# A four-block transformer kernel: memory layer and compressed attention spread beside other TensorE work, last feed-forward chunks token tile outer

## What is computed

```python
# first block, each layer
hf = swiglu(rms_norm(x, g[0]), w_gate[layer, 0], w_up[layer, 0], w_down[layer, 0])
x = x + 0.5 * rms_norm(hf, g[1]);  xn = rms_norm(x, g[2])
x = x + rms_norm(mixer(xn), g[3])
...                                   # second FFN with g[4], g[5]
# memory layer
qk, v, o, gates = split(xn @ w_in)
q, k = split(silu(causal_depthwise_conv(qk, conv_w)))      # 4 taps
hid = h_num / maximum(abs(n_num), exp(-m_t))               # per head
hid = hid * rsqrt(mean(hid * hid) + EPS) * head_g * sigmoid(o)
# second block, layer 0: compressed attention
blocks = t[:, :, win_idx, :] + pos        # 15 blocks of 32 tokens, stride 16
cmp = gelu(flat(blocks) @ w1) @ w2        # once for keys, once for values
o_c = masked_softmax(q @ k_cmp * scale + bias) @ v_cmp
o = sigmoid(g0) * o_c + sigmoid(g1) * o_selected + sigmoid(g2) * o_window
```

## Time and profile before

| | us |
|---|---|
| median of 3 runs | 2490.64 (2482.09 to 2491.22) |
| the profiled execution, its own time | 2498.82 |
| its span from first to last instruction | 2497.0 |
| PE busy | 2196.6 (88%) |
| DVE busy | 1714.2 (69%) |
| ACT busy | 1077.2 (43%) |
| GpSimd (POOL) busy | 711.0 (28%) |

### The profile page before, as it was taken

The page is one execution under the profiler, slowest core; times in us unless marked ns, Lnnn a source line. Parts: engine busy times, 40 slices in busy tenths (PEclk is TensorE's granted clock), DMA queues, the critical chain, the costliest instruction groups (busy, mean ns, idle before and its releaser), DMA issues.

```text
span 2497.0 us, 30819 instructions
## 1 busy us (share of the span) xinstructions
PE 2196.6 (88%) x13056; PEld 1916.5 (77%) x13056; DVE 1714.2 (69%) x1351; ACT 1077.2 (43%) x1097; POOL 711.0 (28%) x350
## 2 busy tenths in 40 slices
PE   7997978998998955899897869999998877999996
PEld 6896958998998944899795758777777556777775
DVE  5897346997998456699723666777774346767766
ACT  4433455334334423433432435655552334645544
POOL 2898004995996000499400000000000000000000
PEclk9998988999999976999897879999998778999998
DMA  9776505876786620678551036787774104877773
GB/s 330 264 261 212 183 23 200 277 258 215 264 270 205 186 86 9 217 264 279 190 158 62 1 118 225 281 286 278 264 245 150 34 18 153 305 260 275 270 255 115
DMA packets 281913, 495.95 MB, mean 199 GB/s; under 512 B 11816, under 2 KB 167576, under 8 KB 281616
## 3 DMA queue, kind: packets, MB, share of 16 engines
q1 hardware_dynamic: 257952, 410.19, 48.9%
q0 software_dynamic: 23552, 82.75, 9.2%
q10 hardware_dynamic: 272, 1.05, 0.1%
HBM read 486.56 MB, written 12.10 MB: 200 GB/s over the span
## 4 chain that ended last, share of the span: by engine, by line
PE 75%; DVE 13%; DMA 5%; ACT 4%; issue 3%; ACTq 0%; DVEq 0%; SPq 0%
PE psum L901 72%; DMA ring<-in_moe_w_up 3%; DVE nrm L1845 3%; DVE low L1845 2%; ACT wh L1505 2%; DMA ring<-in_ffn_w_up 2%; PE psum L961 1%; DVE hl L1845 1%; DVE wide L2225 1%; DVE xl L1845 1%; PE psum L1113 1%; DVE wide L1845 1%; DMA ring<-in_moe_w_down 1%; DMA ring<-in_moe_w_gate 0%; DVE aux L1845 0%
## 5 line engine op out<-in xcount | busy, mean ns | idle before, releaser
L1845 DVE TENSOR_TENSOR low<-ring,wh 128x2048 fp32r<-128x2048 f32 x386 | 1072.5, 2800 | 402.3 <-ACT wh L1505 402.2
L1505 ACT ACTIVATE wh<-ring 128x2048 fp32r<-128x2048 f32 x386 | 733.4, 1906 | 720.0 <-PE psum L901 323.1
L901 PE MATMUL psum<-xh,wh 128*128 128x256 f32 x1832 | 522.3, 285 | 6.7 <-DVE xl L1845 4.3
L901 PE MATMUL psum<-xh,low 128*128 128x256 f32 x1832 | 522.9, 285 | 0.0
L901 PE MATMUL psum<-xl,wh 128*128 128x256 f32 x1832 | 520.7, 284 | 0.0
L712 POOL TENSOR_TENSOR big<-big 128x1024 f32<-128x1024 f32 x144 | 374.7, 2602 | 11.3
L901 PEld LDWEIGHTS psum<-xh,wh 128*128 128x128 f32 x1832 | 353.0, 193 | 12.8 <-issue 8.3
L901 PEld LDWEIGHTS psum<-xl,wh 128*128 128x128 f32 x1832 | 352.0, 192 | 1.5
L901 PEld LDWEIGHTS psum<-xh,low 128*128 128x128 f32 x1832 | 352.2, 192 | 0.0
L901 PE MATMUL psum<-wh,xh 128*128 128x256 f32 (+5 forms) x864 | 279.2, 323 | 11.9 <-DVEq L617 5.8
L901 PE MATMUL psum<-wh,bigr 128*128 128x512 f32 x768 | 255.9, 408 | 23.3 <-DVE hl L1845 23.3
(11 more groups left out here) (326 smaller groups left out, 2536.0 us busy)
## 6 DMA issues: line engine op xcount, KB each, us to landing
ring<-in_moe_w_gate SPq DMA_DIRECT2D x64, 1024.0 KB, 5.3
ring<-in_moe_w_up SPq DMA_DIRECT2D x64, 1024.0 KB, 5.9
ring<-in_moe_w_down SPq DMA_DIRECT2D x64, 1024.0 KB, 5.1
big<-in_ada_w POOLq DMA_DIRECT2D x48, 1024.0 KB, 6.6
ring<-in_ffn_w_gate SPq DMA_DIRECT2D x44, 1024.0 KB, 5.4
ring<-in_ffn_w_up SPq DMA_DIRECT2D x44, 1024.0 KB, 5.5
ring<-in_ffn_w_down SPq DMA_DIRECT2D x44, 1024.0 KB, 5.7
ring<-in_mlstm_w_in SPq DMA_DIRECT2D x16, 1024.0 KB, 5.6
```

The costliest lines, as they stand in the source:

```text
L901: return pe.matmul(out_, lhsT, rhs, start=start, stop=stop, **kw)
L1505: act.activation(wh[n % PARTS][:, 0:w], ring[n % RING][:, 0:w], ACT.Copy).then_inc(high, 1)
L1845: return dve.tensor_tensor(out_, a, b, op)
```

## The change

The memory layer: the gate piece of 16 columns is projected first. The stage `gates` is gone. Its PE part stands behind pieces 2 and 6 of the projection, its ACT and DVE parts between their work on the pieces. The convolution is made for two blocks of 128 channels at a time (`convolve`) as soon as a piece has been copied, in place, and the first tap starts the sum. The output gate gets its Sigmoid as it leaves PSUM. In the head loop ACT also takes the sum of squares of each head's output; DVE multiplies the output gate with the head gain at head 1 and with four heads' outputs at head 6. The tail is left with the other four heads and one scaling by a factor that joins the division and the normalization.

Compressed attention: the stages `compress` and `cmp` are gone, their steps are spread over the pairs of `soft_attention`, which now starts with MoBA. They use PSUM bank 7, so that the scores of token tile 0 have bank 6 alone and PE waits until DVE has read the scores of pair i+1, not of pair i, before it makes those of pair i+2. Four heads share one matmul, by zero-padded keys and a block-diagonal value matrix.

FFN: the last two chunks are done with the token tile outer, the low part of the last piece is made ahead of the last hidden features, and where a `norm` without modulation follows a `residual`, each tile goes through both before the next tile starts.

```diff
-        MLSTM_IN = [256] * 16 + [16]
+        MLSTM_IN = [16] + [256] * 16
...
-                add("gates")
...
-                add("compress", pieces=[("one", w1[half * 1024:half * 1024 + 1024, :].rearrange("(k p) n -> p k n", p=P), GU)
-                add("cmp")
-                add("soft", ("selected", "window", "moba"))
+                add("soft", EVEN_RUN, pieces=[("one", w1[half * 1024:half * 1024 + 1024, :]
...
                 gate_up_products(0)
-                for c in range(chunks):
-                    if c + 1 < chunks:
-                        gate_up_products(c + 1)
-                    down_products(c)
+                for c in range(chunks - 2):
+                    gate_up_products(c + 1)
+                    down_products(c, (0, 1))
+                gate_up_products(chunks - 1)
+                for t in range(TT):
+                    down_products(chunks - 2, (t,), signal=t == 1)
+                    down_products(chunks - 1, (t,))
...
+                    if name == "mlstm" and j == 2:
+                        turn_gates()
+                    if name == "mlstm" and j == 6:
+                        gate_columns()
...
+                    scores_read(*run[0])
                 scores(*run[1])
+                if even:
+                    for part in range(2):
+                        hidden_blocks(s, part)
                 for i, pair in enumerate(run):
                     turn_probs(*pair, 0)
                     turn_probs(*pair, 1)
                     if i + 2 < len(run):
-                        scores_read(*pair)
+                        scores_read(*run[i + 1] if even else pair)
                         scores(*run[i + 2])
+                    if even:
+                        compressed(s, i)
                     values(*pair, 0)
                     values(*pair, 1)
 
-            def gates(s, k):
...
+            def compressed(s, i):
+                if i < 2:
+                    hidden_blocks(s, 2 + i)
+                if i == 3:
+                    pe.wait_ge(comp_act, 1)
+                    for part in range(4):
+                        at = N_U + P * part
+                        last = pe.transpose(psum[:, 7, part * 30:(part + 1) * 30], big[0:30, at:at + P],
+                                            ident[0:30, 0:30])
+                    last.then_inc(comp_pe, 1)
+                if i == 4:
+                    pe.wait_ge(comp_dve, 10)
+                    for v in range(2):
+                        for half in range(2):
+                            g = N_GT + 30 * half + NCMP * v
+                            mm(psum[64 * v:64 * v + 64, 7, 0:NCMP], aux[:, 256 + 64 * half:320 + 64 * half],
+                               big[:, g:g + NCMP], half == 0, half == 1)
+                    for v in range(2):
+                        for half in range(2):
+                            g = N_GV + 64 * (2 * half + v)
+                            last = mm(psum[64 * v:64 * v + 64, 7, 64:128], big[:, g:g + 64],
+                                      aux[:, 384 + 64 * half:448 + 64 * half], half == 0, half == 1)
+                    last.then_inc(comp_pe, 1)
+                if i == 5:
+                    pe.wait_ge(comp_dve, 13)
+                    for g in range(4):
+                        for t in range(TT):
+                            q, at = N_Q + g * T + t * P, 32 * (2 * g + t)
+                            last = mm(psum[:, 7, at:at + 32], big[:, q:q + P], kcmp, True, True)
+                    last.then_inc(cmp_pe, 1)
+                if i == 7:
+                    pe.wait_ge(cmp_act, 1)
                     for t in range(TT):
+                        last = pe.transpose(psum[:, 7, t * P:(t + 1) * P], cS[:, t].rearrange("p h n -> p (h n)"), ident)
+                    last.then_inc(cmp_pe, 1)
+                if i in (8, 9):
+                    t = i - 8
+                    pe.wait_ge(cmp_dve, 2 + t)
+                    mm(psum[:, 7, :], cPT[:, t * P:(t + 1) * P], vblock, True, True).then_inc(cmp_pe, 1)
...
+                    if c == chunks - 1:
+                        high_of("d", c)
                     silu_of_gate(c)
-                    high_of("d", c)
+                    if c < chunks - 1:
+                        high_of("d", c)
...
+            def gates(j):
+                l, f = aux[0:8, A_L:A_L + T], aux[0:8, A_F:A_F + T]
+                if j == 3:
+                    act.wait_ge(gates_dve, 2)
+                    link(act.activation(l, f, ACT.Abs))
+                    link(act.activation(l, l, ACT.Exp, scale=-1.0))
+                    act.activation(l, l, ACT.Ln, bias=ones[0:8, :]).then_inc(gates_act, 1)
+                if j == 5:
+                    act.wait_ge(gates_dve, 8)
+                    act.activation(f, f, ACT.Exp, scale=-1.0).then_inc(gates_act, 1)
+                if j in (6, 8, 10, 12):
+                    g = j // 2 - 3
+                    act.wait_ge(gates_dve, 8 + 16 * (g + 1))
+                    part = big[:, M_PRE + 1024 * g:M_PRE + 1024 * (g + 1)]
+                    act.activation(part, part, ACT.Silu)
 
...
+                        if merged(s + 1):
+                            norm_tile(s + 1, t)
...
+                    if names == EVEN_RUN and i == 2:
+                        act.wait_ge(piece_used, PIECE0[s] + 4)
+                        act.activation(big[0:30, N_U:N_U + 512], psum[0:30, 7, :], ACT.Gelu_apprx_tanh)\
+                            .then_inc(comp_act, 1)
+                    if names == EVEN_RUN and i == 6:
+                        act.wait_ge(cmp_dve, 1)
+                        act.activation(cS, cS, ACT.Exp).then_inc(cmp_act, 1)
...
+                    for t in range(TT):
+                        at = S_MS + 8 * t + h
+                        ins = act.activation(sq[:, P * ((2 * h + t) % 8):P * ((2 * h + t) % 8) + P], psum[:, 4 + h % 2, t * VW:t * VW + P], ACT.Square,
+                                             accum_out=small[:, at:at + 1])
+                    ins.then_inc(ml_act, 1)
...
+            def convolve(c):
+                dve.wait_ge(proj_read, PROJ_AT["mlstm"] + c + 1)
+                for step, tap in enumerate((1, 2, 3, 0)):
+                    for i, acc in enumerate(conv_sum):
+                        m, n = 2 * (c - 1) + i, 8 + 8 * (c - 1) + 2 * step + i
                         w = small[:, S_CONVW + 16 * (3 - tap) + m:S_CONVW + 16 * (3 - tap) + m + 1]
                         src = big_t(M_PRE, m)
+                        dve.wait_ge(gates_dve, n - 1)
+                        if tap == 1:
+                            ins = dve.tensor_scalar(acc[:, 1:T], src[:, 0:T - 1], w, None, ALU.mult)
+                        elif tap:
+                            ins = dve.scalar_tensor_tensor(out=acc[:, tap:T], in0=src[:, 0:T - tap], scalar=w,
+                                                           in1=acc[:, tap:T], op0=ALU.mult, op1=ALU.add)
                         else:
+                            ins = dve.scalar_tensor_tensor(out=src, in0=src, scalar=w, in1=acc, op0=ALU.mult,
...
+                    if h == 1:
+                        output_gates()
+                    if h == 6:
+                        dve.wait_ge(ml_act, 2 * 3 + 3)
+                        gated_outputs(0)
...
+                link(dve.scalar_tensor_tensor(out=den, in0=den, scalar=EPS * P, in1=den, op0=ALU.mult, op1=ALU.mult))
+                tt(den, den, ms, ALU.add).then_inc(ml_dve, 1)
+                gated_outputs(1)
...
+                    tt(nrm[:, t, :].rearrange("p (h w) -> p h w", h=H), raw[:, t, :, 0:P], spread(den[:, t, :], 2, P),
+                       ALU.mult)
...
+            def compressed(i):
+                mx, sums, inv = (small[:, at:at + 16].rearrange("p (t h) -> p t h", t=TT) for at in S_CMP)
+                if i == 3:
+                    dve.wait_ge(comp_pe, 2)
+                    for part in range(4):
+                        to = big[:, N_GV + 64 * part:N_GV + 64 * part + 64].rearrange("p (a n) -> p a n", a=4)
+                        at = 60 + NCMP * part
+                        dve.tensor_copy(to[:, :, 0:NCMP], spread(psum[:, 7, at:at + NCMP], 1, 4))
+                    dve.tensor_copy(big[:, N_GT:N_GT + 60], psum[:, 7, 0:60]).then_inc(comp_dve, 1)
+                if i == 4:
+                    dve.wait_ge(comp_pe, 3)
                     for v in range(2):
+                        rows, at = slice(64 * v, 64 * v + 64), N_KCMP + 16 * v
+                        dve.tensor_copy(big[rows, at:at + NCMP], psum[rows, 7, 0:NCMP]).then_inc(comp_dve, 1)
+                    tt(vblock.rearrange("p (h w) -> p h w", h=H), spread(psum[:, 7, 64:128], 1, H),
+                       spread(const[:, C_BLOCK:C_BLOCK + H], 2, 64), ALU.mult).then_inc(comp_dve, 1)
+                if i == 5:
+                    dve.wait_ge(cmp_pe, 1)
+                    ps = psum[:, 7, 0:256].rearrange("p (g t v n) -> p g t v n", g=4, t=TT, v=2)
+                    for v in range(2):
```

(26 more changed lines are left out.)

460 lines of the change are left out of this document (205 added, 255 removed).

## The result

| | us |
|---|---|
| before, median (2482.09 to 2491.22) | 2487.98 |
| after, median (2405.41 to 2411.27) | 2408.32 |
| ratio, 95% interval | 0.9675 (0.9655 to 0.9695) |
| predicted | 2423 (2408 to 2444) |

The change saves 79.7 us where I predicted 67.5. The direction was right and the saving 12.2 us short.

A forecast was written before the change was run, and what follows sets the result against it. PE was taken as the bound, with time to win only where it stands still or does small work. Terms -36.7 + 5.4 + 0.6 - 11.1 - 22.7 - 5.0 + 2.0 = -67.5 gave 2423 us from the median 2490.6, range 2408 to 2444.

The forecast's parts named there:

- rival (2): Head loop: Square isn't in Exp's table, so every head loads twice, +16 us, 2439 us in all; chance 0.05.
- I had +0.6: Head loop: DVE's added work +2.6 us, less 2.0 for a better clock behind dense work; bounds -2 and +5.
- I had -11.1: Memory layer's tail: the PE gap of 18.8 us shrinks, ending at 976.8 instead of 988.0; bounds -13 and -8.
- I had 22.7: Compressed attention: the 48.3 us go, less 0.7 for meeting and 24.9 of growth; saving bounds 9 and 29.
- I had -1.8: Second and third FFN ends: tile 1 no longer waits 2.1 us for tile 0's norm, -1.8 us each.
- +1.0 as foretold: After the two output projections: tile 1 is 2.65 us later and saves 2.1 less 0.5, +1.0 each.
- Together -5.0 and +2.0, so -3.0: FFN ends -5.0 us and output projections +2.0 us, a net saving of 3.0; bounds -8 and +4.
- The last down product now has only 2.8 us of cover for the hidden features, which take 2.0: enough: FFN ends: 2.8 us of the last down product were held to cover the hidden features' 2.0.
- priced at -1.4: First FFN end: low part moved ahead ends it 2.9 us earlier; pads' flip holds back transposes 1.5.
- I take 4 us at half speed in place of full, 2.0.: Memory projection: the wide piece behind the narrow front piece starts at the low clock, costing 2.0 us.
- rival (4): Memory projection: narrow piece in front keeps TensorE at 1.2 GHz throughout; all 16 wide pieces give 2515 us; chance 0.01.
- rival (3): Nothing is late and the clock stays up through loop and pairs: saving 79 us, 2411 us; chance 0.13.

The follow-up runs named there:

- after_shift: Changed kernel with the table of constants 8 columns wider still, so the buffers behind it lie 32 bytes further: 2405.48 us, ratio to before 0.9669.
- ffn_only: Kernel before with the feed-forward part of the change alone: 2488.42 us, ratio to before 1.0017.
- no_merge: Changed kernel without merging residual and norm tile by tile; order of the last two chunks and early low part stay: 2406.95 us, ratio to before 0.9682.
- after_again: Changed kernel as it is, profiled a second time: 2403.76 us, ratio to before 0.9677.

## Why the prediction was right and wrong

**Right.** `gates` is gone to a boundary of 0.7. The spread work keeps PE's pace. Timeline of after: the table load and Exp of the gates' chain, DVE's work on one piece, and the wait of PE ahead of piece 6:

```profile
833.50 1.28 ACT L1742 ACT_TABLE_LOAD   x1
834.80 0.42 ACT L1742 ACTIVATE aux<-aux 8x256 f32<-8x256 f32 x1
...
845.32 0.61 DVE L2324 TENSOR_SCALAR wide<-big,small 128x255 f32<-128x255 f32 x2
845.84 1.66 DVE L2326 SCALAR_TENSOR_TENSOR wide<-big,small,wide 128x254 f32<-128x254 f32 x4
847.42 0.87 DVE L2329 SCALAR_TENSOR_TENSOR big<-big,small,wide 128x256 f32<-128x256 f32 x2
848.21 2.28 DVE L1910 TENSOR_TENSOR low<-ring,wh 128x2048 fp32r<-128x2048 f32 x1
...
845.55 0.36 PE L934 MATMUL psum<-xh,wh 128*128 128x256 f32 x1 [1.63 <-DVE low L1910]
```

The convolution of a piece takes 3.0 (845.32 to 848.29) and the low part 2.3, so 5.2 of 5.7 (I had 2.9 and 5.2), and the wait is 1.63 (1.5). Exp starts 1.30 after its table load began: by this row too there is no further drain. This speaks against the 1380 ns that the Trainium skill gives for it (ScalarE: Activation LUTs, "What ACT_TABLE_LOAD costs"). The head loop, one cycle of ACT:

```profile
918.61 0.52 ACT L1831 ACTIVATE wide<-wide 128x384 f32<-128x384 f32 x1 [2.79 <-DVE wide L2359]
919.04 0.37 ACT L1821 ACTIVATE wide<-psum 128x258 f32<-128x258 f32 x1
919.31 0.27 ACT L1825 ACTIVATE squares<-psum 128x128 f32<-128x128 f32 x1
...
921.01 0.52 ACT L1831 ACTIVATE wide<-wide 128x384 f32<-128x384 f32 x1 [1.08 <-DVE wide L2359]
```

2.40 us a cycle, and squares come between two Exps with no table load: rival (2) is dead. That the whole loop came so near to before's (27.77 for 27.68, I had +0.6) was in part luck. The clock was low for 6.8 us of it in this profile; in `after_shift`, which does the same work, for 20.5, and there the loop took 29.9 (columns of rows 2):

```profile
912.86:942.76 29.90, 26.96 (x96) 19.76 (x96) 18.97 (x37) 16.41 (x48) 0.58 (x1) 0.66 0.16 54
```

The tail:

```profile
935.90 4.48 DVE L1910 TENSOR_TENSOR low<-ring,wh 128x2048 fp32r<-128x2048 f32 x2
...
941.02 1.28 DVE L1910 TENSOR_TENSOR wide<-wide,biasT 128x512 f32<-128x512 f32 x2
...
942.63 2.36 DVE L1910 TENSOR_TENSOR nrm<-wide,small 128x1024 f32<-128x1024 f32 x2
945.08 3.67 PE L994 MATMUL psum<-const,nrm 128*128 128x128 f32 x16 [8.11 <-DVEq L626]
```

Two low parts to 940.4, gating of half the heads, one scaling: 8.11 us of stop, -10.7 where I had -11.1 (my own terms, 988.0 to 976.8, give -11.2). In the pairs the first transposes come 14.0 us after the stage starts (13 to 15 foretold), behind two weight pieces:

```profile
1269.72 0.25 PE L1252 MATMUL psum<-const,aux 32*128 32x32 f32 x1 [0.72 <-ACTq L626]
...
1275.85 3.64 PE L934 MATMUL psum<-ring,big 128*30 128x256 f32 x16 [1.58 <-DVE big L1910]
...
1283.71 0.85 PE L1147 MATMUL psum<-const,wide 128*128 128x128 f32 x6 [0.30 <-PE psum L934]
```

The stretch is 24.7 shorter by the first pair of profiles, I had 22.7. At the merged ends the stop is split as foretold:

```profile
793.92 1.09 PE L994 MATMUL psum<-const,nrm 128*128 128x128 f32 x8 [1.03 <-DVE nrm L1983]
...
799.47 1.97 PE L994 MATMUL psum<-const,nrm 128*128 128x128 f32 x8 [4.45 <-DVE nrm L1983]
```

From the end of the network's products to the next product it is 9.2 us in place of 10.79: -1.6, I had -1.8. At the output projections it is 11.76 for 10.79, +1.0 as foretold.

**Wrong, the feed-forward ends: the clock behind a split stop.** The step "Together -5.0 and +2.0, so -3.0" failed. The delays at the merged ends and at the output projections were right to 0.2, and the sign of the sum was wrong: +4 alone, 6 to 9 in company. I priced how long PE stops and not at which level it starts again. Low clock until 5 us into a stage costs 2 to 2.5. It was new at two places: the fourth network (203.2 for 201.1 in the means) and, in `ffn_only`, the start of the memory layer (low until 4.8 us behind the restart, in before back ahead of it). At the second and third networks, where before's work mostly has the low clock too, the means fell by 1.4 and 0.5 where I had 1.8 each.

**Wrong, the cover of the last hidden features.** "The last down product now has only 2.8 us of cover for the hidden features, which take 2.0: enough" left out that the low part of 2.3 now stands ahead of them. In `no_merge` PE waits 1.6 and 2.2 there; in after's profile no such wait shows (up to 1.2 in the others with these ends), and the later clock there is the loss. At the first network, priced at -1.4, the stage grew by 2.3 in the means (225.2 for 222.9): all transposes waited for both norms, and PE stood 19.4 us.

**Wrong size, the narrow piece in front.** "I take 4 us at half speed in place of full, 2.0." It was 15.4 us at half speed. The narrow piece took 10.4 for 6.85 and the next 7.8 for 5.7, 5.6 in all, and the whole projection grew by 8.2 (98.2 to 106.4) where I had 5.4. I had named a low clock from the narrow piece on as rival (4), but for the whole projection and at a chance of 0.01: I saw that the projection ran at 1.00 from its first piece, but that piece was wide. The row that could have told is the narrow piece at its old place, 0.77.

**Missing, the code loads.** This is the largest error: 13 to 14 us by the times of the two runs, of the 21 from the first experts on. By single profiles of the two it is 11 and 19, and profiles of the same work differ by up to 15 there (1020 to 1034, 998 to 1013), so how much of the 21 is left for something else stays open. No rival had it; rival (3) gave the same total by another mechanism, a clock that stays up in loop and pairs. It rose in the loop of after's profile (0.69 to 0.88) but not in that of `after_shift` (0.66), level with after in time, and the touched stages saved 60 and not 79: that mechanism is not it.

The account: -67.5, +7 for the feed-forward part, +3 for the narrow piece, -2 for compressed attention, is -59.5, which is the 60 of the touched stages; -21 behind them gives the 80 measured. The total was near by luck: two errors of opposite sign met, 8 too much for the touched stages and 21 missing behind them.

## What to carry to other kernels

Price a split or moved stop by the clock at which TensorE starts again, and by which work it starts with: leave wide passes first, as they stood here before, or turn a narrow product round so that its long side moves. Where a chain of waits has transfers in it, as in the experts' stages, a change far ahead can shift when code loads hit them; judge such a change by runs that hold the number of TensorE's instructions, and don't credit that part to the edit. A work order that shortens a stop by 1.6 us can lose 2 to 2.5 behind it: measure each part alone before keeping it.

## What the runs showed of the hardware

- A code load of 16 KB took one DMA engine for 1.0 us. The weight piece of 1 MB issued 89 us into the second experts' stage landed 5.9 to 6.3 us after its issue where such a load met it, and 5.1 to 5.5 where none did. 116 instructions more at the head of TensorE's queue cost 13 us beside their own 4.3, up to 2 ms behind them; 140 in the other kernel won 14.
- Empty instructions left no trace in the program; increments of a semaphore cost 0.04 to 0.05 us each (4.3 for 116, 7.5 for 140).
- 48 passes of 16 columns with 128 stationary columns ran at 0.213 us each at 1.2 GHz and did not bring the clock up; 24 passes of 256 columns with 16 stationary ones began at the same pace, and the clock rose behind the eighth.
- Two executions of the same program differ by where the clock is low: attention took 126.7 us in after and 129.3 in `after_again`, and the memory layer's head loop 27.8 at a granted clock of 0.88 in after and 29.9 at 0.66 in `after_shift`, whose buffers alone lie elsewhere.
